# First projection products by 384 tokens, with the first weights loaded ahead of the modulation slice

## The reference, cut to what matters

```
sh1, sc1, g1, sh2, sc2, g2 = split(silu(cvec) @ w_mod + b_mod, 6)     # adaLN, w_mod 1024 x 6144
h = rmsnorm(x, norm1_g) * (1 + sc1) + sh1
q, k, v, bg, cg, xin = split(h @ w_in)                                # w_in 1024 x 2304
```

## Time and profile before

| | |
|---|---|
| runs | 902.39, 905.57, 909.11 us (median 905.57) |
| profiled execution | 903.66 us, its span 901.7 us |
| mean granted TensorE clock | 0.987 |
| TensorE busy | 860.7 us (95%) |
| VectorE, ScalarE, GpSimd busy | 682.2, 462.2, 224.0 us |

### The profile page before, as it was taken

The page is one execution under the profiler, slowest core; times in us unless marked ns, Lnnn a source line. Parts: engine busy times, 40 slices in busy tenths (PEclk is TensorE's granted clock), DMA queues, the critical chain, the costliest instruction groups (busy, mean ns, idle before and its releaser), DMA issues.

```text
span 901.7 us, 12088 instructions
## 1 busy us (share of the span) xinstructions
PE 860.7 (95%) x4445; PEld 683.1 (76%) x4445; DVE 682.2 (76%) x1018; ACT 462.2 (51%) x694; POOL 224.0 (25%) x206
## 2 busy tenths in 40 slices
PE   4999999999998999999999889999999999999996
PEld 3789999999996555578888657777777777777653
DVE  5457876968856777456888657988888988888678
ACT  6541211111125777544453517877777767776533
POOL 1000000000024777522012131422332233222141
PEclk9899999999999999999999979999999999999999
DMA  9731626424200113042121579999999999998296
GB/s 367 313 117 45 218 64 243 165 93 164 68 29 29 48 40 109 8 164 89 52 92 49 199 260 403 382 379 381 381 379 370 372 382 371 361 367 337 103 376 256
DMA packets 39923, 194.52 MB, mean 216 GB/s; under 512 B 10071, under 2 KB 11031, under 8 KB 22967
## 3 DMA queue, kind: packets, MB, share of 16 engines
q1 hardware_dynamic: 30296, 174.76, 51.6%
q0 software_dynamic: 9568, 19.00, 5.6%
HBM read 181.99 MB, written 26.41 MB: 231 GB/s over the span
## 4 chain that ended last, share of the span: by engine, by line
PE 73%; DVE 9%; DMA 7%; ACT 4%; issue 3%; POOL 2%; POOLq 0%; SPq 0%; DVEq 0%; ACTq 0%
PE PS L968 9%; PE PS L970 8%; PE PS L972 8%; DMA w_gu<-in_w_gu 5%; PE PS L2417 5%; PE PS L2418 5%; PE PS L2419 5%; PE PS L2451 4%; PE PS L1081 3%; PE PS L1112 3%; PE PS L1728 3%; PE PS L1132 3%; PE PS L1730 2%; PE PS L1729 2%; PE PS L2406 2%
## 5 line engine op out<-in xcount | busy, mean ns | idle before, releaser
L2222 DVE TENSOR_TENSOR gu_lo<-w_gu,gu_hi 128x2048 fp32r<-128x2048 f32 x62 | 141.9, 2289 | 29.8 <-ACT gu_hi L2108 29.8
L2108 ACT ACTIVATE gu_hi<-w_gu 128x2048 fp32r<-128x2048 f32 x62 | 118.9, 1917 | 62.2 <-DMA w_gu<-in_w_gu 62.1
L968 PE MATMUL PS<-h_hi,w_hi 128*128 128x384 f32 (+1 forms) x432 | 148.3, 343 | 2.5 <-DVE h_lo L677 1.9
L970 PE MATMUL PS<-h_lo,w_hi 128*128 128x384 f32 (+1 forms) x432 | 147.0, 340 | 0.0
L972 PE MATMUL PS<-h_hi,w_lo 128*128 128x384 f32 (+1 forms) x432 | 146.4, 339 | 0.0
L2417 PE MATMUL PS<-gu_hi,xT_hi 128*128 128x512 f32 x256 | 103.3, 403 | 1.2 <-DVE xT_lo L2281 1.2
L2418 PE MATMUL PS<-gu_lo,xT_hi 128*128 128x512 f32 x256 | 100.4, 392 | 0.0
L2419 PE MATMUL PS<-gu_hi,xT_lo 128*128 128x512 f32 x256 | 100.2, 391 | 0.0
L2052 POOL DMA_INDIRECT y_rows<-yrows,tab x31 | 37.3, 1205 | 209.6 <-DVE yrows L2254 209.6
L968 PEld LDWEIGHTS PS<-h_hi,w_hi 128*128 128x128 f32 x432 | 81.8, 189 | 8.9 <-issue 7.6
L970 PEld LDWEIGHTS PS<-h_lo,w_hi 128*128 128x128 f32 x432 | 82.3, 190 | 0.0
(11 more groups left out here) (274 smaller groups left out, 1737.1 us busy)
## 6 DMA issues: line engine op xcount, KB each, us to landing
w_gu<-in_w_gu SPq DMA_DIRECT2D x64, 1024.0 KB, 13.4
w_d<-in_w_down SPq DMA_DIRECT2D x32, 1024.0 KB, 12.6
wm<-in_w_mod SPq DMA_DIRECT2D x16, 1024.0 KB, 5.4
w_raw<-in_w_in SPq DMA_DIRECT2D x18, 512.0 KB, 6.5
yt<-y_rows SPq DMA_DIRECT2D x9, 1024.0 KB, 14.9
xt<-in_x_all SPq DMA_DIRECT2D x9, 512.0 KB, 3.5
h_rows<-h SPq DMA_DIRECT2D x9, 512.0 KB, 2.7
y_all<-yt SPq DMA_DIRECT2D x9, 512.0 KB, 2.8
```

What stands on the lines that cost most here:

```text
L968: pe.matmul(o, w_hi[b][:, k, :], h_hi[:, k, tok], start=k == 0, stop=False)
L970: pe.matmul(o, w_hi[b][:, k, :], h_lo[:, k, tok], start=False, stop=False)
L2108: act.activation(gu_hi[n % 2][:, h, :], w_gu[:, n % 3, h, :], ACT.Copy).then_inc(s_hi, 1)
L2222: dve.tensor_tensor(gu_lo[:, n % 3, h, :], w_gu[:, n % 3, h, :], raw(gu_hi[n % 2][:, h, :]), ALU.subtract).then_inc(s_lo, 1)
```

## The change

Nothing of what is computed changes, only order and sizes at the start. The rows come in five loads (tile 0, 1-2, 3-4, 5, 6-8); tiles 3 and 4 are put aside, in the room of the rotary tables, since xs lies where h_lo is written (which is why `consumed` on VectorE waits for a tile's square and norm before h_lo covers it). On the SP queue chunk 0 and slice 0 come right after tiles 0 to 2, then the small constants, bias, tiles 3-4, chunk 1, tile 5, slice 1, tiles 6-8. TensorE turns tiles 0 to 2, sums slice 0, and does the products of chunks 0 and 1 for blocks k = 0 to 3 on the first 384 tokens only, two blocks of one chunk and then two of the other in turn; then it turns tiles 3 and 4, sums slice 1, turns tile 5, and does the second 384 tokens of the same blocks; blocks 4 to 7 go by 768 tokens as before. ScalarE and VectorE make h_hi and h_lo of blocks 0 to 3 in two pieces of 384 accordingly, the squares, norms and keeps of tiles 3 to 5 coming between. More products that nobody reads are put in: 24 ahead of the first turn, 4 after it, 2 after the sum of slice 0, 4 after its columns (before there were 4 in all, there). The banks of the turns and of the slice-0 sum are others, and the semaphore counts grow by 4.

```diff
@@ -170,7 +170,7 @@
         s_folding = sem("s_folding")
         s_modrows = sem("s_modrows")
         s_cpad = sem("s_cpad")
-        s_xload = [sem(f"s_xload{i}") for i in range(4)]
+        s_xload = [sem(f"s_xload{i}") for i in range(5)]
         s_wm = [sem(f"s_wm{i}") for i in range(2)]
         s_gemv = sem("s_gemv")
         s_modp = sem("s_modp")
@@ -249,7 +249,11 @@
 
             def turn_banks(t):
 
-                return (2 * (t % 2), 2 * (t % 2) + 1) if t < EARLY else (2, 5)
+                return (1 + 3 * (t % 2), 2 + 3 * (t % 2)) if t < EARLY else (2, 5)
+
+            def head_piece(k, hi):
+
+                return k + 1 if hi == TGN else k + 5
 
             def turned_rows(t):
 
@@ -265,6 +269,16 @@
             NEXTRA = MODS - 4
             tables = sb2("tables", [P, 2 * N_LAT + 2 * P])
             cosT, sinT = tables[:, 0:N_LAT], tables[:, N_LAT:2 * N_LAT]
+            xs_aside = tables[:, 0:2 * D].rearrange("p (t n) -> p t n", t=2)
+
+            def x_tiles(lo, hi):
+
+                return xs_aside if lo in XPARTS[2] and hi == 5 else xs[:, lo:hi, :]
+
+            def x_tile(t):
+
+                return xs_aside[:, t - 3, :] if XPART[t] == 2 else xs[:, t, :]
+
             xin_sb, u_sb, y_sb = work
             ck_raw = tables[:, 2 * N_LAT:2 * N_LAT + P]
             nat = tables[:, 2 * N_LAT + P:2 * N_LAT + 2 * P]
@@ -276,7 +290,8 @@
             HALVES_AT |= {13: [(7, 0)], 14: [(7, 1)]}
             EARLY = 6
             HEAD = EARLY * P
-            XPART = [0, 0, 1, 1, 2, 2, 3, 3, 3]
+            XPARTS = [(0, 1), (1, 3), (3, 5), (5, 6), (6, 9)]
+            XPART = [p for p, (lo, hi) in enumerate(XPARTS) for _ in range(lo, hi)]
             TAILS = [(0, slice(HEAD, N_LAT)), (1, slice(N_LAT, T))]
             NCONV = 3 * CG
             V_PARTS = [4, 4, 1]
@@ -340,24 +355,25 @@
                                  ).then_inc(s_wmh[h], 16)
 
                 def rows_in(part):
-                    tiles_in = slice([0, 2, 4, 6][part], [2, 4, 6, 9][part])
-                    sp.dma_start(xs[:, tiles_in, :], a["x_all"][:, tiles_in, :]
+                    lo, hi = XPARTS[part]
+                    sp.dma_start(x_tiles(lo, hi), a["x_all"][:, lo:hi, :]
                                  ).then_inc(s_xload[part], 16)
 
                 sp.dma_start(craw[:], a["cvec"]).then_inc(s_cvec, 16)
                 rows_in(0)
                 sp.dma_start(ident[:], a["ident"]).then_inc(s_ident, 16)
                 rows_in(1)
+                chunk(0)
+                first_slice(0)
                 sp.dma_start(consts[:, 0:32], a["percol"]).then_inc(s_const, 16)
                 sp.dma_start(selcol[:], a["selcol"]).then_inc(s_const, 16)
-                rows_in(2)
-                first_slice(0)
-                chunk(0)
                 sp.wait_ge(s_fill, 4)
                 sp.dma_start(modA[0:2, :], a["b_mod"][:, 0:2 * D]).then_inc(s_mod_bias, 16)
+                rows_in(2)
                 chunk(1)
+                rows_in(3)
                 first_slice(1)
-                rows_in(3)
+                rows_in(4)
                 first_slice(2)
                 first_slice(3)
                 chunk(2)
@@ -472,7 +488,7 @@
                     act.wait_ge(s_xload[XPART[t]], 16)
                     if t >= 2:
                         act.wait_ge(s_xn, t - 1)
-                    act.activation(sqj[:], xs[:, t, :], ACT.Square,
+                    act.activation(sqj[:], x_tile(t), ACT.Square,
                                    accum_out=ssq[b][:, 0:1]).then_inc(s_sq, 1)
                     act.wait_ge(s_sq, t + 1)
                     act.activation(ssq[b][:, 1:2], ssq[b][:, 0:1], ACT.Sqrt, bias=eps_col[:],
@@ -489,8 +505,8 @@
                         last = act.activation(dst, src, ACT.Copy)
                     last.then_inc(s_kept, 1)
 
-                def h_head(k):
-                    act.activation(h_hi[:, k, 0:HEAD], cat[:, k, 0:HEAD], ACT.Copy,
+                def h_head(k, lo=0, hi=HEAD):
+                    act.activation(h_hi[:, k, lo:hi], cat[:, k, lo:hi], ACT.Copy,
                                    scale=s1[:, 0, k:k + 1]).then_inc(s_hhi, 1)
 
                 def h_tail(k):
@@ -508,23 +524,27 @@
                 square(1)
                 square(2)
                 keep(0)
+                keep(2)
+                act.wait_ge(s_kept, 2)
+                act.wait_ge(s_keptd, 1)
+                act.wait_ge(s_s1, 2)
+                for k in range(4):
+                    h_head(k, 0, TGN)
                 square(3)
                 square(4)
-                keep(2)
                 square(5)
                 keep(4)
                 act.wait_ge(s_kept, 3)
                 act.wait_ge(s_keptd, 3)
-                act.wait_ge(s_s1, 2)
                 for k in range(4):
-                    h_head(k)
+                    h_head(k, TGN, HEAD)
                 square(6)
                 square(7)
                 act.wait_ge(s_s1, 4)
                 h_head(4)
                 square(8)
+                h_head(5)
                 keep(6)
-                h_head(5)
                 h_head(6)
                 h_head(7)
                 keep(8)
@@ -639,7 +659,7 @@
                     dve.wait_ge(s_rs, t + 1)
                     if t >= 2:
                         dve.wait_ge(s_xT, t - 1)
-                    dve.tensor_scalar(xn[b][:], xs[:, t, :], ssq[b][:, 0:1], None,
+                    dve.tensor_scalar(xn[b][:], x_tile(t), ssq[b][:, 0:1], None,
                                       ALU.mult).then_inc(s_xn, 1)
 
                 def low(n):
@@ -672,10 +692,10 @@
                     dve.wait_ge(s_sq, t + 1)
                     dve.wait_ge(s_xn, t + 1)
 
-                def h_head(k):
-                    dve.wait_ge(s_hhi, k + 1)
-                    dve.scalar_tensor_tensor(h_lo[:, k, 0:HEAD], cat[:, k, 0:HEAD],
-                                             s1[:, 0, k:k + 1], raw(h_hi[:, k, 0:HEAD]),
+                def h_head(k, lo=0, hi=HEAD):
+                    dve.wait_ge(s_hhi, head_piece(k, hi))
+                    dve.scalar_tensor_tensor(h_lo[:, k, lo:hi], cat[:, k, lo:hi],
+                                             s1[:, 0, k:k + 1], raw(h_hi[:, k, lo:hi]),
                                              ALU.mult, ALU.subtract).then_inc(s_hlo, 1)
 
                 def h_tail(k):
@@ -697,29 +717,36 @@
                 norm(1)
                 norm(2)
                 keep(1)
+                low(0)
+                dve.wait_ge(s_mod_bias, 16)
+                mod_row(0, 7)
+                dve.wait_ge(s_const, 32)
+                scales(0)
+                dve.wait_ge(s_s1, 2)
+                dve.wait_ge(s_kept, 2)
+                dve.wait_ge(s_keptd, 1)
+                consumed(2)
+                h_head(0, 0, TGN)
+                h_head(1, 0, TGN)
+                low(1)
+                h_head(2, 0, TGN)
+                h_head(3, 0, TGN)
                 norm(3)
                 norm(4)
                 keep(3)
                 norm(5)
                 keep(5)
-                dve.wait_ge(s_mod_bias, 16)
-                mod_row(0, 4)
-                low(0)
-                dve.wait_ge(s_const, 32)
-                scales(0)
-                dve.wait_ge(s_s1, 2)
                 dve.wait_ge(s_kept, 3)
                 dve.wait_ge(s_keptd, 3)
-                consumed(5)
-                h_head(0)
-                low(1)
-                h_head(1)
+                h_head(0, TGN, HEAD)
                 mod_row(1, 7)
-                h_head(2)
-                h_head(3)
+                h_head(1, TGN, HEAD)
+                h_head(2, TGN, HEAD)
                 scales(1)
+                h_head(3, TGN, HEAD)
                 norm(6)
                 dve.wait_ge(s_s1, 4)
+                consumed(5)
                 h_head(4)
                 norm(7)
                 consumed(6)
@@ -988,30 +1015,47 @@
                                          sums_of[p % 2][:, j, :], start=True, stop=True)
                     last.then_inc(s_gemv2, 1)
 
+                def unread(of, n):
+                    for _ in range(n):
+                        pe.matmul(PS[:, 0, 0:P], of[:], of[:], start=True, stop=True)
+
+                pe.wait_ge(s_fill, 3)
+                unread(ones, 24)
                 pe.wait_ge(s_ident, 16)
-                for t in range(EARLY):
-                    turn(t)
+                turn(0)
+                unread(ones, 4)
+                turn(1)
+                turn(2)
                 pe.wait_ge(s_cpad, 1)
-                mod_sum(0, 4)
+                mod_sum(0, 7)
+                unread(ones, 2)
                 pe.wait_ge(s_const, 32)
                 mod_cols(0, 6)
-                for _ in range(2):
-                    pe.matmul(PS[:, 5, 0:P], ident[:], ident[:], start=True, stop=True)
-                    pe.matmul(PS[:, 5, 0:P], ident[:], ident[:], start=True, stop=True)
+                unread(ones, 4)
```

(34 more changed lines are left out.)

## The result

The changed kernel takes 906.22 us (median of 21 runs, 902.61 to 912.28), the kernel before 903.67 us (21 runs, 901.60 to 909.11): ratio 1.0031, 95% interval [1.0017, 1.0046]. I forecast 903.0 and a gain of 1.6 us; it is a loss of 2.6 us. It lies within the 1% that I called the same, and inside the range, but with the other sign.

What follows compares the result with a forecast made beforehand. TensorE, busy 95% of the span, bounds the kernel. Start +6.0, lower clock gone +2.6, turns -2.9 and waits -4.15 give 1.6 us gained; 904.6 less 1.6 is 903.0 us, range 899.5 to 908.0.

Steps and rivals of the forecast that it cites:

- Earlier start: Start of the kernel: slice 0's sum waits for three tiles only, first projection product at 19.95 us, 6.0 us earlier.
- turns: Turns 3 to 5, moved behind the first products, add 2.9 us to TensorE's work there.
- waits: TensorE waits in the head: 0.55 for chunk 1, 2.65 before the second part, 0.8 and 0.15 later; -4.15 us.
- the wait at k = 4: Second part of the head: TensorE waits for h_lo 4, queued behind norm 6 on VectorE; 0.8 us lost.
- Lower clock gone ... +2.6: Start: the profiled low-clock stretch goes, so 12 products and a sum run at full clock; 2.6 us gained.
- The forecast that the clock would hold: Head: granted clock 1.00 from 15 to 60 us, giving the 1.6 us gain; chance 0.40.
- Rival A: Head: clock still falls after thin stretch or wait; one fall about 906, both about 909; chance 0.35 (0.25 and 0.10).
- The unread products at nothing: Start: the new unread products cost nothing; the 24 leading ones end at 9.6 us; at worst 1.8 us lost.
- Rival B: Start: the 24 unread products run slow throughout, turn 2 at 16, products from 21.8; -0.2 us, 904.8; chance 0.07.
- C: Head: waits at turn 5 and k = 4 are half those worked out; +3.5 us, about 901; chance 0.08.
- Rival D: Behind the head: the gain at 57.45 is lost in later low-clock stretches; either sign, up to 3 us; chance 0.10.
- the DMA is costed at nothing: Start: one more SP issue and small loads behind slice 0 cost nothing, unless a small load is late.

Runs made afterwards that it cites:

- e5: Changed kernel with turn 5 right behind turn 4, into banks 6 and 7, ahead of the slice 1 sum: 901.33 us, ratio 0.9995 to the kernel before.
- e3: Changed kernel without the 24 leading unread products, the 4 after turn 0 and the 2 after the slice 0 sum: 906.94 us, ratio 1.0043 to before.
- e1: Changed kernel with 12 more unread products behind turn 5, in the wait before the second 384 tokens: 903.09 us, ratio 0.9999 to the kernel before.
- e9: Changed kernel with a longer wait: VectorE copies turn 5's banks twice more ahead of keep 5; 909.41 us, ratio 1.0070 to the kernel before.
- e8: Changed kernel with the columns of slice 1 moved into the wait behind turn 5: 903.58 us, ratio 1.0006 to the kernel before.
- e4: Changed kernel timed again with no edit: 905.71 us, ratio 1.0028 to the kernel before.
- e7: Kernel before, old order, with 24 leading unread products and nearly all gaps up to the first product filled with more: 900.63 us, ratio 0.9974.
- e10: e7 timed again: 899.86 us, ratio 0.9970 to the kernel before.
- e11: e7 without the 24 unread products ahead of the first turn: 904.17 us, ratio 1.0010 to the kernel before.

## Why the prediction was wrong, point by point

**Earlier start, turns, waits: right.** First product 19.96 for 19.95; the long wait 2.78 for 2.65; the wait at k = 4 0.43 for 0.8; last third at full clock near 55.7 for 55.85.

**"Lower clock gone ... +2.6": the step that failed.** It credited the change with the whole fall that the profile of before showed, and with no fall of its own. The fall of before was one execution's: 48 of its 93 runs have a mean clock of 0.989 or more. Over the runs, and over the whole span, the clock term is not +2.6 but -1.5 us (12.12 lost for 10.58). The rest of my sum, 1.6 - 2.6 = -1.0, was right: at full clock the last third starts near 55.7 in the changed kernel and near 54.8 in the one before, 0.9 us later, and the runs' clocked time says 1.1 ± 0.3. So the order alone loses a microsecond, and the 4.1 us between +2.6 and -1.5, with 0.5 outside the span, make the difference between the gain of 1.6 and the loss of 3.1 in the means. e5 shows what the order's loss hangs on: with 1.9 us off the wait before the second part, the time from the first product to the last third is 34.04 us for 35.77 in e3. The six microseconds won at the start are spent on the three turns and on that wait.

**The forecast that the clock would hold: wrong in the mean.** Rival A had the mechanism and its place; I gave it 0.35 against 0.40. That its time for one fall (906) is the measured median is partly luck: it took 1.2 us from a base of 904.6, where the kernel before measured 903.67 and the loss was 2.6, and it too counted on the +2.6. That the wait has a part in it is shown by e1 and e5: filled or shortened, 3 to 3.5 us of the 12.1 come back, each with an error of 1.0. e9 points the same way but isn't clear, and e8 leaves 2 us of the wait and loses 10.5. The runs list only the mean clock, so how much of it is lost in the head and how much behind 60 us is known for the profiles alone. What A missed is the spread: behind the wait the clock was low for 3.4 us in one profile, 10.4 in another, not at all in a third (e3), with the same instructions from turn 3 on.

**The unread products at nothing: right** for the changed kernel (e3). They ended at 8.5 in the first profile (9.6 forecast), and full speed there is shown by the turns behind them, 8 in 1.04 us for 1.95 without the lead. The rule that I took from the Trainium skill (TensorE: Matmul & The Clock Gate, What's actually happening), that activity releases the throttle, agrees with that. **Rival B is out** (turn 2 ends at 12.8, not 16), and so is C (2.78 us of wait). **Rival D** is real as scatter: from the last third to the end it took 842.0 to 848.2 us in the thirteen profiles, the largest in e4 and the smallest in e7 and e10, so that 2 us of what those two profiles gain lie behind the head.

**A cover that was not priced.** Before, the sum of slice 0 waited for turn 5, with slice 0 already there (it starts with no wait for it in the earlier trace rows); now it waits for the data, and an execution with slow loads (15.85 in e4, 14.07 in the first profile) passes 1.8 us on. I wrote that the DMA is costed at nothing, and looked only at the small loads.

**Open.** 0.5 us of the difference lies outside the span (2.44 against 1.95). It is there in the kernels with the new load order except in 5 of the 6 runs of e9, and in 8 of the 12 of e11, which has the old one; what it is the runs don't tell. How often the clock falls by the thin stretch from 13 to 20 us and how often by the wait alone was not separated run by run.

## What to carry to other kernels

Set a forecast against the distribution of the kernel before, not against its profiled execution: where that shows a stretch at the lower clock, work out the sum at full clock for both, and the clock as its own term. A reordering that starts TensorE six microseconds sooner gains nothing if the work is only put behind and a wait opens with nothing to put into it; look for the chain (copy, scale, subtract) between the last piece of old work and the first of the new, and put other work there. In the old order unread products, in the gaps and 24 in front, were worth 0.3%, where the reordering was worth nothing; without the 24 in front the first real work ran at half speed and the gain was gone.

## What I had not expected of the hardware

The same program has executions with a mean clock from 0.991 to 0.979, and their spans differ by 9.7 us (900.1 to 909.8). The profile reads 1.00 for the first microseconds where eight transposes take 1.95 us for 1.04: a clock reading of 1.00 at the start says nothing until a duration confirms it.
